# The low half of act moved ahead of the fourth split of the down weights

## The reference

```python
for layer in range(DEPTH):
    x = x + mixer(rms_norm(x, attn_norm[layer]))
    x = x + hierarchical_moe(rms_norm(x, ffn_norm[layer]), ...)

# inside hierarchical_moe, D_MODEL = 1024, D_EXPERT = 512
for e in range(N_EXPERTS):
    act = jax.nn.silu(hf @ w_gate[e]) * (hf @ w_up[e])
    y = y + combine[:, e:e + 1] * (act @ w_down[e])
```

## Time and profile before

| | us |
|---|---|
| median of 3 runs | 1289.53 |
| lowest and highest run | 1288.2, 1292.21 |
| the profiled execution | 1285.25 |
| its span in the trace | 1283.5 |

### The profile page before, as it was taken

How to read it: one execution, slowest core, us unless ns; L and a number is a source line. 1 busy time by engine, 2 the same in 40 slices (tenths; PEclk the granted TensorE clock), 3 DMA queues, 4 the chain that set the end, 5 groups by cost and what they waited for, 6 DMA issues and landing times.

```text
span 1283.5 us, 16959 instructions
## 1 busy us (share of the span) xinstructions
PE 1180.3 (92%) x5788; PEld 898.5 (70%) x5788; DVE 914.7 (71%) x1251; ACT 674.1 (53%) x843; POOL 97.3 (8%) x128
## 2 busy tenths in 40 slices
PE   5999879999799999999878999999979999999986
PEld 4776669878776766766646688887876666667663
DVE  4646668656579888888967247646558898888886
ACT  4335651134347778777733242132426777787862
POOL 1120000000010000000030000001001100000003
PEclk9999999999899999999989999999979999999998
DMA  6231110123599999999860240113169999999955
GB/s 221 91 89 66 66 66 1 66 73 125 187 331 363 366 385 390 384 382 384 332 220 1 70 136 15 66 66 131 66 257 303 368 381 381 383 391 385 381 203 209
DMA packets 129423, 281.75 MB, mean 220 GB/s; under 512 B 18945, under 2 KB 19457, under 8 KB 129361
## 3 DMA queue, kind: packets, MB, share of 16 engines
q1 hardware_dynamic: 119680, 246.98, 53.2%
q0 software_dynamic: 5888, 20.97, 5.3%
q10 hardware_dynamic: 3792, 12.98, 2.7%
HBM read 262.05 MB, written 18.87 MB: 219 GB/s over the span
## 4 chain that ended last, share of the span: by engine, by line
PE 57%; DVE 25%; issue 9%; ACT 6%; POOL 1%; DMA 1%; DVEq 1%; ACTq 0%; SPq 0%
PE PS L1109 16%; PE PS L1111 15%; PE PS L1110 15%; DVE expert_w_low L1824 10%; PE PS L1213 4%; DVE group_low L1612 2%; PE PS L1343 2%; ACT weight_high L870 1%; PE PS L1148 1%; DVE xgT_low L1832 1%; DVE act L1845 1%; DVE score_max L1743 1%; DVE G L1502 1%; PE PS L1323 1%; DVE hT_low L1596 1%
## 5 line engine op out<-in xcount | busy, mean ns | idle before, releaser
L1824 DVE TENSOR_TENSOR expert_w_low<-expert_w,weight_high 128x1024 fp32r<-128x1024 f32 x368 | 426.5, 1221 | 75.0 <-ACT weight_high L870 71.3
L870 ACT ACTIVATE weight_high<-expert_w 128x1024 fp32r<-128x1024 f32 x384 | 375.5, 1049 | 69.6 <-PE PS L1111 61.9
L1109 PE MATMUL PS<-weight_high,xgT_high 128*96 128x512 f32 x512 | 204.5, 399 | 2.6 <-DVEq L1834 2.6
L1111 PE MATMUL PS<-weight_high,xgT_low 128*96 128x512 f32 x512 | 203.2, 397 | 0.0
L1110 PE MATMUL PS<-expert_w_low,xgT_high 128*96 128x512 f32 x512 | 202.1, 395 | 0.0
L1109 PE MATMUL PS<-group_high,hT_high 128*128 128x512 f32 x416 | 172.2, 414 | 13.9 <-DVEq L1599 9.5
L1111 PE MATMUL PS<-group_high,hT_low 128*128 128x512 f32 x416 | 165.3, 397 | 0.0
L1110 PE MATMUL PS<-group_low,hT_high 128*128 128x512 f32 x416 | 165.0, 397 | 0.0
L1109 PE MATMUL PS<-weight_high,actT_high 128*96 128x512 f32 x256 | 104.3, 407 | 19.4 <-DVEq L1882 18.9
L1612 DVE TENSOR_TENSOR group_low<-group_w,group_high 128x1024 fp32r<-128x1024 f32 x68 | 80.8, 1223 | 43.4 <-ACT group_high L894 39.5
L1109 PEld LDWEIGHTS PS<-weight_high,xgT_high 128*96 128x96 f32 x512 | 83.3, 163 | 36.0 <-DVEq L1834 2.7
(11 more groups left out here) (251 smaller groups left out, 1469.9 us busy)
## 6 DMA issues: line engine op xcount, KB each, us to landing
expert_w<-in_moe_w_gate SPq DMA_DIRECT2D x32, 2048.0 KB, 13.7
expert_w<-in_moe_w_up SPq DMA_DIRECT2D x32, 2048.0 KB, 15.0
expert_w<-in_moe_w_down SPq DMA_DIRECT2D x32, 2048.0 KB, 13.5
group_w<-in_even_w_in SPq DMA_DIRECT2D x6, 2048.0 KB, 7.8
group_w<-in_odd_w_in SPq DMA_DIRECT2D x6, 2048.0 KB, 8.1
y_rows<-yb ACTq DMA_DIRECT2D x30, 384.0 KB, 6.1
group_w<-in_even_w_out SPq DMA_DIRECT2D x2, 2048.0 KB, 7.9
h_rows<-h SPq DMA_DIRECT2D x8, 512.0 KB, 11.3
```

Of the source, the lines that this page charges most:

```text
L870: act_(hi, w, ACT.Copy).then_inc(w_hi, 1)
L1109: pe.matmul(out, ah, bh, start=first, stop=False)
L1111: return pe.matmul(out, al, bh, start=False, stop=final)
L1824: tt(lo, w, hi.bitcast(F32), ALU.subtract).then_inc(w_lo, 1)
```

## The change

VectorE's block asks for three of the four low splits of the down weights, then computes `actT_low`, and then asks for the fourth. It applies to all blocks but the last of each layer, where the down weights are split elsewhere.

```diff
                     if not last:
-                        low(DOWN, b, par)
+                        low(DOWN, b, par, range(SPLITS - 1))
                     key = ("actT", l)
                     ve.wait_ge(actTh_ready, b + (l * NE + 1))
                     link(tt(actTl[:].rearrange("p k n -> p (k n)"), bank(key)[:, 0:4 * CAP],
...
                     ve.sem_inc(actT_ready, 1)
                     ve.sem_inc(bk.freed(key), 1)
                     if not last:
+                        low(DOWN, b, par, range(SPLITS - 1, SPLITS))
                         low(UP, b, par)
```

## The result

| | before | after |
|---|---|---|
| median of 3 runs, us | 1289.53 | 1271.41 |
| lowest and highest | 1288.2, 1292.21 | 1268.1, 1272.14 |
| profiled execution, span | 1285.25, 1283.5 | 1268.1, 1266.3 |
| mean clock granted to TensorE | 0.968 | 0.967 |

The ratio of the times is 0.9849, interval 0.9813 to 0.9886. I had forecast 14.4, with 1270.5 as the low end of the range. The direction and the mechanism held; two sizes did not.

The account below looks back on a forecast made before the run. TensorE's waits for actT_low, 18.9 us, were taken as the bound. Blocks 0 and 1, the loop and block 14 give 12.8 us, the clock 1.57: 14.4 us, so 1275.1 us against 1289.53, range 1270.5 to 1282.

Parts of the forecast that it names:

- What is waited for: Down product in the expert loops: both beats of the two-beat pattern are released by actT_low, TensorE starting 0.19 us after its end.
- 1.14 us for passing one split: VectorE, 15 of 16 blocks per layer: actT_low starts 1.14 us earlier by passing the fourth low split.
- Blocks 0 and 1, 1.76 per layer: First two blocks of each layer: block 1's down product comes 1.76 us earlier, block 0's gain included.
- The floor of the gap: Loop blocks 3 to 12, ahead of the down product: 0.69 and 0.78 us remain, gaining 3.8 and 3.2 us by layer.
- the way up to 15.3: Sum of the gains without the clock if the loop's gaps fall to 0.61 us, instead of 12.8.
- The clock: Block 14's down product: wait shrinks from 3.22 to 2.4 us, one of two clock drops gone, 1.57 us, bounds 0 and 3.1.
- Fourth split, up splits: VectorE behind actT_low: fourth split waits 0.25 us, is done 3.4 us before need; up splits not later, their idle stays.
- DMA: Gate weights late in layer 0's loop: landing 17.2 us after issue, 1.1 us left over, transfers costed at nothing.
- The gap of 0.79: Rival: loop gaps stop at the even beat's 0.79 us, TensorE's register work and transposes limiting; 1277.9 us, chance 0.15.
- Late weights: Rival: expert weights land late, taking layer 0's loop gain and the clock's share; 1280.5 us, chance 0.08.
- The gain coming back on the up splits: Rival: TensorE waits for the up splits instead, only the two blocks 14 gain, 2.3 us; 1287.2 us, chance 0.06.
- VectorE standing before actT_low: Slower rival: actT_high, due only 0.22 us ahead, comes late and delays actT_low and the fourth split; 1305 us, chance 0.03.

## Why the prediction was right in kind and wrong in size

*What is waited for.* Right. The product stood behind actT_low in both beats, and with it earlier both fell to one period of 17.67 us.

*1.14 us for passing one split.* Right: block 14, the one place where nothing else binds, gave 1.13 and 1.14 when it was changed alone. In after it gave 1.24 and 1.15 together with block 13.

*Blocks 0 and 1, 1.76 per layer.* Right: 1.79 and 1.80.

*The floor of the gap.* This step failed. I put the floor between 0.61 and 0.69 in layer 0, 0.61 and 0.78 in layer 1, and took the upper ends, "since the register work stands between the transposes and the product". That was an argument from the order of the instructions, not from a row; the one row without any lateness, block 2, said 0.61. Measured is 0.61 in every loop block of both layers, and the run with two splits behind confirms it as the floor. The 0.08 and 0.17 of extra delay in before were paid only while the value waited for came last. Price of the error: 4.70 + 5.03 - 7.0 = 2.7 us, close to the 2.5 that I had given as the way up to 15.3. Why the register work costs nothing now, the runs do not show: it may be done while the transposes run, but no experiment put it elsewhere.

*The clock.* The term was mis-sized: 1.57 taken, 3.1 measured at block 14. I took the middle of 0 and 3.1, one fall of two gone, for want of a reason either way. In four profiles of after no layer fell there, in two of before both did. But the term looked at block 14 only. In after's first profile a fall at block 15 took 1.57 us back, so the two together gave 1.55, what I had forecast, and that by luck. Over all the profiles before has 5 falls at the two blocks in 4 layers and after 3 in 8: 1.75 falls less per execution, which at 1.56 us each is some 2.7 us, my estimate. At block 14 the shorter wait comes with fewer falls (2 of 26 up to 2.8 us, 7 of 8 from 3.2). The length does not decide by itself: 2.36 us brought no fall in eight cases and a fall in two, and block 15's 1.38 us one in 19 of 34. What else decides stays open.

*The two together* make 18.8 where I had 14.4, or 17.3 with the fall at block 15, which is what the span fell by. That the ratio stands for 19.5 is within its interval. The range's low end of 1270.5 stood 0.4 above the measured 1270.1, although my own bounds already gave 18.4 us and 1271: both ends came true at once, and the range left the runs' own spread no room below.

*Fourth split, up splits.* Right. The split's own wait was 0.32 us, not 0.25; it was done 3.0 us ahead of its need, where I had 3.4. One sign did not come: I had said that the idle ahead of the up splits stays, and in block 7 it fell from 0.93 to 0.35 us. VectorE's idle ahead of splits, for ScalarE's halves, fell from 71.3 us to 29.6 over the span: the cover is thinner, not gone.

*DMA.* Right in effect: nothing waited. But I reckoned with the old 17.2 us, and it was 21.1. The need moved 5.0 us nearer (625.10 to 620.12) and the issue 4.4, so 2.5 us are left of 7.0 (625.10 - 618.1). The gate loads of the last loop blocks took 19.0, 19.8, 20.5 and 21.1 us to land. By these numbers my estimate is that the cover would have lasted three to four more blocks at 17.67 us, and that TensorE would then have begun to wait for loads.

*Rivals.* The gap of 0.79 is refuted by 0.61. Late weights: no wait on a load. The gain coming back on the up splits: no such wait. VectorE standing before actT_low: not in after, where the margin is 0.80 us in block 7 and 0.60 in block 8, not the 0.22 that I had reckoned. With two splits behind actT_low it starts and is still free. With four it takes most of the gain away, at 0.55 to 0.58 us a loop block; what I had not counted is the idle ahead of the up splits, which it uses up first.

## What to carry to other kernels

An operand's part that the consumer needs three quarters later should not stand ahead of the part it needs first; what the move costs is found by the idle that the engine has just behind. Take the floor of a gap from a block that nothing releases late, not from the instructions written in it, and let a term with two possible values reach the range as those two values. When a clock fall has gone from one place, count the falls at the next waits too before you book the gain. When a wait has gone, look for the next small chain beside it: one more split and two spread chains gave another 4.6 us by the ratios, about a quarter of the change.

## What the runs showed of the hardware

- The same 2.36 us of idle on TensorE was followed by full clock in eight cases and by the lower level in two, and 3.27 us by either in one execution.
- An issue of a load by SyncE took 4.51 us instead of 0.37. The landing times of the gate loads grew from 10.7 us at block 0 to 21.1 at the end of layer 0's loop, and the issues grew long from 490 us on: the last load takes longer to land than a block lasts (17.67). In before they grew too, from 10.7 to 17.2 us against blocks of 17.85 and 18.48, and every issue of the loop took 0.37 or 0.38 us.
- Behind the 1.38 us of idle at block 15 the clock fell in 19 of 34 cases; in 17 of them the wait at block 14, some 15 us earlier, had brought none. In before and the three kernels with the change in some blocks only it was 1 of 10.
- A fall in a down product cost between 1.3 and 2.8 us (first to last start 6.69 to 8.20 us, against 5.39).
